# Routed experts of a decoder layer: weight pieces of 2048 columns, x turned after four contraction tiles, activations turned one block later

## The reference

```python
def expert_block(args):                      # xblk: up to 128 tokens of expert e
    xblk, e = args
    hid = jax.nn.silu(xblk @ w_gate[e]) * (xblk @ w_up[e])
    return hid @ w_down[e]
yb = lax.map(expert_block, (xb, block_e)).reshape(n_rows, d)
y = jax.ops.segment_sum(yb * row_w[:, None], row_tok, num_segments=t + 1)
```

## Time and profile before

| | |
|---|---|
| median of 3 runs | 2982.65 us (2980.33 to 2990.67) |
| the profiled execution, device time | 2996.13 us |
| its span in the trace | 2994.6 us |
| stretch with the experts' gate and up matmuls | 1879.7 to 2922.6 us |
| TensorE busy in the whole span | 84% |
| VectorE, ScalarE, GpSimd busy in the whole span | 61%, 42%, 28% |

### The profile page before, as it was taken

One profiled execution on the slowest core, in us unless ns is written; L12 is line 12 of the kernel. 1 busy time (PEld: TensorE's weight loads), 2 busy tenths in 40 slices (PEclk: granted clock), 3 DMA queues, 4 the chain that ended last, 5 costly groups with the idle time before them and its releaser, 6 DMA issues. The chain is left out here.

```text
span 2994.6 us, 38917 instructions
## 1 busy us (share of the span) xinstructions
PE 2519.6 (84%) x12384; PEld 2055.2 (69%) x12385; DVE 1819.8 (61%) x2399; ACT 1264.9 (42%) x1673; POOL 841.4 (28%) x895
## 2 busy tenths in 40 slices
PE   7989998998999899969978831799898988989891
PEld 6768777777877777847857721577777776777680
DVE  3346887787788655536546621666656667656744
ACT  3343453354345333334222100566656566555640
POOL 2012111221211111100002071444444444444442
PEclk8989999999999999989989875899999999999995
DMA  5423345442323353263543245778888889878954
GB/s 114 67 41 63 68 45 54 64 58 50 74 54 50 71 78 78 57 206 111 169 161 105 68 40 106 258 242 269 257 251 257 264 288 299 248 220 248 309 126 140
DMA packets 244044, 428.85 MB, mean 143 GB/s; under 512 B 26393, under 2 KB 150809, under 8 KB 243935
## 3 DMA queue, kind: packets, MB, share of 16 engines
q1 hardware_dynamic: 209566, 343.36, 42.6%
q0 software_dynamic: 34368, 84.02, 12.1%
HBM read 366.16 MB, written 93.58 MB: 154 GB/s over the span
## 5 line engine op out<-in xcount | busy, mean ns | idle before, releaser
L58 PE MATMUL dn_pj<-x_hi,dn_hi 128*128 128x512 f32 x1024 | 440.6, 430 | 4.1 <-PEq L83 2.2
L60 PE MATMUL dn_pj<-x_hi,dn_lo 128*128 128x512 f32 x1024 | 412.4, 403 | 0.0
L59 PE MATMUL dn_pj<-x_lo,dn_hi 128*128 128x512 f32 x1024 | 411.4, 402 | 0.0
L1007 DVE SCALAR_TENSOR_TENSOR uc_half<-u_in,par,uc_half 128x512 f32<-128x512 f32 x480 | 383.2, 798 | 13.1
L2247 DVE TENSOR_TENSOR e_lo<-e_raw,e_hi 128x1024 fp32r<-128x1024 f32 x256 | 337.1, 1374 | 73.0 <-ACT e_hi L2190 65.3
L58 PE MATMUL gu_ps<-e_hi,xg_hi 128*128 128x512 f32 x744 | 326.2, 438 | 56.2 <-DVE xg_lo L2252 33.7
L2190 ACT ACTIVATE e_hi<-e_raw 128x1024 fp32r<-128x1024 f32 x256 | 253.2, 1052 | 162.5 <-DMA e_raw<-in_w_gate_e_dram 130.3
L60 PE MATMUL gu_ps<-e_hi,xg_lo 128*128 128x512 f32 x744 | 307.3, 413 | 0.0
L59 PE MATMUL gu_ps<-e_lo,xg_hi 128*128 128x512 f32 x744 | 306.7, 412 | 0.0
L1146 POOL TENSOR_TENSOR a_lvl<-a_t,lvl_mask 128x512 f32<-128x512 f32 x112 | 167.7, 1514 | 353.1 <-PE dn_a L685 223.5
L60 PEld LDWEIGHTS dn_pj<-x_hi,dn_lo 128*128 128x128 f32 x1024 | 199.4, 195 | 46.4
(11 more groups left out here) (343 smaller groups left out, 5172.0 us busy)
## 6 DMA issues: line engine op xcount, KB each, us to landing
e_raw<-in_w_gate_e_dram SPq DMA_DIRECT2D x128, 512.0 KB
e_raw<-in_w_up_e_dram SPq DMA_DIRECT2D x128, 512.0 KB
e_raw<-in_w_down_e_dram SPq DMA_DIRECT2D x128, 512.0 KB
dn_raw<-in_w_in_dram SPq DMA_DIRECT2D x64, 512.0 KB
gate_rows<-qkv_next SPq DMA_DIRECT2D x16, 512.0 KB, 3.6
br_raw<-in_w_oa_dram SPq DMA_DIRECT2D x16, 512.0 KB
br_gate<-gate_rows SPq DMA_DIRECT2D x32, 256.0 KB, 4.2
br_raw<-in_w_ob_dram SPq DMA_DIRECT2D x16, 512.0 KB
```

What stands on the lines that cost most here:

```text
L58: nc.tensor.matmul(out, w_hi, x_hi, start=first, stop=False)
L59: nc.tensor.matmul(out, w_hi, x_lo, start=False, stop=False)
L60: return nc.tensor.matmul(out, w_lo, x_hi, start=False, stop=last)
L1007: ins = stt(out=uc[:], in0=u_in[:, t:t + HALF], scalar=w, in1=uc[:], op0=ALU.mult, op1=ALU.add)
```

## The change

It does five things in `experts`.

1. `raw` becomes three pieces of 2048 columns: gate and up of tiles 0 to 3, gate and up of tiles 4 to 7, and both halves of down. SP still issues six DMAs of 512 KB for an expert, two into each piece, and waits once for each piece. ScalarE and VectorE split a piece with one instruction.
2. Down weights are split one expert ahead instead of two, with semaphores of their own, and `down` waits for them. SP loads gate and up of expert e before down of e-1.
3. TensorE turns the next block's x after tiles 0 to 3. The activations are turned at the same place of the next block; the wait for `hid_s` stands in front of gate|up. Inside a group of three experts the two register loads of the next expert stand after the x transposes.
4. ScalarE's order in a block: piece 0, hi of the activations of the block before, first half of x, piece 1, silu, second half of x, piece 2, `y_move` of the block before.
5. VectorE's order: piece 0, lo of the activations, first half of x, `hidden`, second half of x, pieces 1 and 2.

At the start, only gate and up of experts 0 and 1 and down of expert 0 are split ahead of the loop. The rest of the program is as it was. GpSimd's program differs by the names of the register loads alone.

```diff
...
-            PIECES = 6
+            GU = 2
             BUFS = 3
-            SLOTS = 6
             LAG = 4
-            raw = [sb(ctx, f"e_raw{q}", [P, 4 * FF]) for q in range(SLOTS)]
+            raw = [sb(ctx, f"e_raw{i}", [P, 2, 4 * FF]) for i in range(GU + 1)]
...
-                if i < 4:
-                    ks, w = slice(4 * (i // 2), 4 * (i // 2) + 4), i % 2
-                    return raw[i][:].rearrange("p (k f) -> p k f", k=4), wh[j][:, ks, w, :], wl[j][:, ks, w, :]
-                return raw[i][:], dh[j][:, i - 4, :], dl[j][:, i - 4, :]
+                if i < GU:
+                    wkf = lambda w: w[j][:, 4 * i:4 * i + 4, :, :].rearrange("p k w f -> p w k f")
+                    return raw[i][:].rearrange("p w (k f) -> p w k f", k=4), wkf(wh), wkf(wl)
+                return raw[i][:], dh[j][:], dl[j][:]
...
-                def load(e, first):
-
-                    for i in range(PIECES):
+                def load_gate_up(e, first):
+
+                    for i in range(GU):
                         if not first:
-                            sp.wait_ge(lo_s, e * PIECES + (i + 1 - SLOTS))
-                        r = piece(0, i)[0]
-                        if i < 4:
-                            w = (a["w_gate_e"], a["w_up_e"])[i % 2]
-                            k0 = 4 * (i // 2)
-                            sp.dma_start(r, w[0, bass.ds(e, 1)].rearrange("o (p k) f -> p (o k) f", k=KT)
-                                         [:, k0:k0 + 4, :]).then_inc(w_in[i], 16)
-                        else:
-                            sp.dma_start(r, a["w_down_e"][0, bass.ds(e, 1)].rearrange("o (c p) n -> p (o c) n", p=P)
-                                         [:, i - 4, :]).then_inc(w_in[i], 16)
-
-                load(0, True)
-                with sp.Fori(1, E) as e:
-                    load(e, False)
+                            sp.wait_ge(lo_s, e * GU + (i + 1 - GU))
+                        for n, w in enumerate((a["w_gate_e"], a["w_up_e"])):
+                            src = w[0, bass.ds(e, 1)].rearrange("o (p k) f -> p (o k) f", k=KT)[:, 4 * i:4 * i + 4, :]
+                            sp.dma_start(raw[i][:, n, :].rearrange("p (k f) -> p k f", k=4), src).then_inc(w_in[i], 16)
+
+                def load_down(e, first):
+
+                    if not first:
+                        sp.wait_ge(dlo_s, e)
+                    for n in range(2):
+                        src = a["w_down_e"][0, bass.ds(e, 1)].rearrange("o (c p) n -> p (o c) n", p=P)[:, n, :]
+                        sp.dma_start(raw[GU][:, n, :], src).then_inc(w_in[GU], 16)
+
+                load_gate_up(0, True)
+                load_down(0, True)
+                load_gate_up(1, False)
+                with sp.Fori(2, E) as e:
+                    load_gate_up(e, False)
+                    load_down(e - 1, False)
+                load_down(E - 1, False)
...
-                def down(j, gb):
+                def down(e, j, gb):
+                    pe.wait_ge(dlo_s, e + 1)
                     pe.wait_ge(hl_s, gb + 1)
                     pe.wait_ge(y_ready, gb + LAG)
...
                 def hid_t(gb):
-                    pe.wait_ge(hid_s, gb + 1)
...
-                def blk(e, j, j_prev, gb, first):
-
-                    pe.wait_ge(xl_s, gb * 2 + 1)
-                    if first:
-                        pe.wait_ge(lo_s, e * PIECES + 2)
-                    gate_up(j, range(0, 4))
-                    pe.wait_ge(xl_s, gb * 2 + 2)
-                    if first:
-                        pe.wait_ge(lo_s, e * PIECES + 4)
-                    gate_up(j, range(4, 6))
-                    transposes(gb + 1)
-                    gate_up(j, range(6, 8)).then_inc(gu_done, 1)
-                    if j_prev is not None:
-                        down(j_prev, gb - 1)
-                    hid_t(gb)
-
-                def expert(e, j, nth, more):
-                    nb, base = plan(pe, e)
-                    blk(e, j, (j + BUFS - 1) % BUFS if not isinstance(e, int) or e > 0 else None, base, True)
-                    with pe.If(nb > 1):
-                        with pe.Fori(1, nb) as b:
-                            blk(e, j, j, base + b, False)
+                def run(experts):
+                    nb, base = blocks(pe, experts[0][0]), first_block(pe, experts[0][0])
+                    for i, (e, j, _) in enumerate(experts):
+                        following = experts[i + 1][0] if i + 1 < len(experts) else None
+                        loaded = []
+
+                        def blk(b, gb, first):
+                            prev = not first or not isinstance(e, int) or e > 0
+                            if prev:
+                                pe.wait_ge(hid_s, gb)
+                            pe.wait_ge(xl_s, gb * 2 + 1)
+                            if first:
+                                pe.wait_ge(lo_s, e * GU + 1)
+                            gate_up(j, range(0, 4))
+                            if prev:
+                                hid_t(gb - 1)
+                            pe.wait_ge(xl_s, gb * 2 + 2)
+                            transposes(gb + 1)
+                            if first:
+                                if following is not None:
+                                    loaded.extend((blocks(pe, following), first_block(pe, following)))
+                                pe.wait_ge(lo_s, e * GU + 2)
+                            gate_up(j, range(4, 8)).then_inc(gu_done, 1)
+                            if prev and first:
+                                down(e - 1, (j + BUFS - 1) % BUFS, gb - 1)
+                            elif prev:
+                                down(e, j, gb - 1)
+
+                        expert(pe, e, nb, base, blk)
+                        if following is not None:
+                            nb, base = loaded
...
-                    act.wait_ge(w_in[i], (nth * BUFS + j) * 16 + 16)
-                    A(h, r, ACT.Copy).then_inc(hi_s, 1)
+                    act.wait_ge(w_in[i], (nth * BUFS + j) * 32 + 32)
+                    A(h, r, ACT.Copy).then_inc(hi_s if i < GU else dhi_s, 1)
...
-                def blk(gb, prev, split):
-
-                    split(0, 1, 2, 3)
-                    act.wait_ge(gu_done, gb + 1)
-                    A(sg[:], gu[:, 0, :], ACT.Silu).then_inc(sg_s, 1)
-                    for b in range(2):
-                        act.wait_ge(t_done, gb * 2 + 5 + b)
-                        x_hi(b)
-                    if prev:
-                        y_move(gb - 1)
-                    act.wait_ge(ht_done, gb + 1)
-                    A(hh[:], ht[:], ACT.Copy).then_inc(hh_s, 1)
-                    split(4, 5)
...
+                def run(experts):
+                    for e, j, nth in experts:
+                        nb, base = blocks(act, e), first_block(act, e)
+
+                        def blk(b, gb, first):
+                            def split(i):
+                                ahead = 2 if i < GU else 1
+                                if first and (not isinstance(e, int) or e + ahead < E):
+                                    hi((j + ahead) % BUFS, nth + (j + ahead) // BUFS, i)
+
+                            prev = not first or not isinstance(e, int) or e > 0
+                            split(0)
+                            if prev:
+                                hid_hi(gb - 1)
+                            act.wait_ge(t_done, gb * 2 + 5)
+                            x_hi(0)
+                            split(1)
+                            act.wait_ge(gu_done, gb + 1)
+                            A(sg[:], gu[:, 0, :], ACT.Silu).then_inc(sg_s, 1)
+                            act.wait_ge(t_done, gb * 2 + 6)
+                            x_hi(1)
+                            split(2)
+                            if prev:
+                                y_move(gb - 1)
+
+                        expert(act, e, nb, base, blk)
...
-                def blk(e, b, gb, split):
-                    split(0, 1, 2, 3)
-                    dve.wait_ge(sg_s, gb + 1)
-                    v.scalar_tensor_tensor(out=hid[:], in0=sg[:], scalar=self.wt_tab[:, bass.ds(e * NT + b, 1)],
-                                           in1=gu[:, 1, :], op0=ALU.mult, op1=ALU.mult).then_inc(hid_s, 1)
-                    x_lo(gb + 1, 0)
-                    x_lo(gb + 1, 1)
+                def hid_lo(gb):
...
+                def run(experts):
+                    for e, j, _ in experts:
...
+                            split(0)
+                            if not first or not isinstance(e, int) or e > 0:
+                                hid_lo(gb - 1)
+                            x_lo(gb + 1, 0)
+                            dve.wait_ge(sg_s, gb + 1)
+                            v.scalar_tensor_tensor(out=hid[:], in0=sg[:], scalar=self.wt_tab[:, bass.ds(e * NT + b, 1)],
+                                                   in1=gu[:, 1, :], op0=ALU.mult, op1=ALU.mult).then_inc(hid_s, 1)
```

(57 more changed lines are left out.)

52 lines of the change are left out of this document (28 added, 24 removed).

## The result

The changed kernel takes **3071.3 us** (median of 4 runs, 3055.6 to 3074.9) against 2981.5 us for the kernel before in the same comparison: a ratio of **1.029, interval 1.025 to 1.032**. The forecast was 2957 us, range 2905 to 3000 us. It is wrong in sign and outside the range.

A forecast was written before the change was run, and what follows sets the result against it. TensorE set a floor of 858 us, with the splitting engines binding runs of one-block experts. Terms 23 - 30 - 9 - 7 - 3 = -26 us, from a median of 2982.65, gave 2957 us, range 2905 to 3000.

The forecast's parts named there:

- first to first: Silu-to-silu steps in runs of one-block experts: 35 steps, from 12.7 to 13.4 us each, +23 us.
- out of a run: Step from the last block of a one-block-expert run to a later block: 15 steps at 8.4 us, -30 us.
- later to first: Step from an expert's later block to the next expert's first block: 25 steps at 10.0 us, -9 us.
- lone first to later: Step from a first block outside such runs to a later block: 11 steps at 9.45 us, -7 us.
- Down starts about 1 us late, covered by the same loop: TensorE's down matmuls: `hid_lo` ready only after piece 0's remainder, about 1 us late, at no extra cost.
- The loop: Piece 1 freed, loaded, hi, silu, `hidden`, second x half, lo, freed: 13.4 us, with 7.5 from freed to full.
- well over 100: Sign of being right: ScalarE's wait for weights' DMA grows from 34 us to this, in front of the piece-1 copy.
- The slower rival: Piece 1's wait ahead of silu, its second half full only 8.8 us after freeing: 3002 us, chance 0.27.
- The start: Before the first silu: two pieces of 1024 fewer stand ahead, 2 to 4 us, taken as -3 us.
- the count of waits costs nothing: SP: same six DMAs but three waits instead of six, no cost; it already waits 434 us for VectorE.
- The third rival: TensorE's register loads left bare, 1.1 us in 17 or so first blocks, 19 us: 2976 us, chance 0.13.

The follow-up runs named there:

- a_1024: The changed kernel's order with six pieces of 1024 columns, each half with its own load, hi copy, subtraction and semaphore: ratio 1.013 to the kernel before.
- a_y_later: The changed kernel with `y_move` taken one block later on ScalarE, behind the activations' hi part and first half of x, ahead of piece 1 and silu: ratio 1.017.
- a_1024_y_pl: a_1024_y with GpSimd reading the next expert's registers behind the store of its first block, instead of ahead of the next gather: ratio 0.987, 2942.8 us.
- a_x6: The changed kernel with the x transposes back behind tile 5 and the register loads ahead of the wait for x: ratio 1.031.
- a_lo_halves: The changed kernel with VectorE's subtraction of each 2048-column piece made as two of 1024: ratio 1.025.
- a_p1: The changed kernel with ScalarE splitting piece 1 after silu and the second half of x: ratio 1.027.
- b_2048: The kernel before with three pieces of 2048 columns alone, in the old order, down still two experts ahead: ratio 1.014.
- b_2048_lo: b_2048 with each subtraction made as two of 1024 columns: ratio 1.001 to the kernel before.
- a_y_lo: The edits of a_lo_halves and a_y_later together on the changed kernel; loads, hi copies and semaphores still by 2048: ratio 1.009.
- a_pair: The changed kernel with hi copies and subtractions by halves of 1024 with own semaphore counts; SP still loads and frees by 2048: ratio 1.021.
- best_loads: a_1024_y_pl with TensorE's register loads of the following expert back in front of its first block, instead of behind the x transposes: ratio 0.986.
- b_pl: The kernel before with GpSimd's register loads placed behind the store: ratio 0.995.
- a_1024_y: The edits of a_1024 and a_y_later together on the changed kernel: ratio 0.994.

## Why the prediction was wrong

The steps between silus, sorted as in the prediction, from each profile's own starts:

| us | first to first (35) | out of a run (15) | later to first (25) | lone first to later (11) | all 92 |
|---|---|---|---|---|---|
| before | 446 | 156 | 259 | 111 | 1030 |
| forecast | 469 | 126 | 250 | 104 | 1007 |
| after | 470 | 163 | 290 | 121 | 1103 |
| a_1024 | 448 | 154 | 293 | 109 | 1064 |
| a_y_later | 448 | 180 | 271 | 116 | 1072 |
| a_1024_y_pl | 403 | 164 | 252 | 106 | 981 |

(The forecast's 1007 is 1030.5 with its four terms, 23 - 30 - 9 - 7.)

**Later to first: the step that failed.** I put "`y_move` is then at about +3.5 to +4", on the ground that GpSimd "was late, since its copy waits for the x transposes" and would start 1.4 us earlier. In the trace above it is at +7.7 (2090.12 against 2082.45), and on average over all 26 such steps (the table leaves one out) at +5.7, where the kernel before has +4.1. The rest of the reckoning held: 5.9 us of ScalarE's work and gaps stand between `y_move` and silu, and 5.7 + 5.9 is the 11.6 us that these steps take. So the term was 40 us too little for the 25 steps.

The store that `y_move` waits for is not issued 1.4 us earlier but 2.3 us later: 1.5 us ahead of silu on average, where the kernel before has 3.8 us (its 19 such steps with this wait). From the issue to `y_move` it takes no longer, 7.1 us against 8.4. GpSimd's loop has grown in two places. With the transposes no longer the last to come, its copy waited 185 us for the gather's landing (a_x6: moving them back changes nothing that can be measured). And I costed the 2048-column subtraction on VectorE alone, where on GpSimd it lengthened idx_gather from 298 to 715 ns, late_rows 423 to 641, idx_scatter 207 to 499 and x_gather 1289 to 1567, some 1.2 us for each block. The second is not what keeps these steps long, though: in a_lo_halves the copies are short and the store is issued at -3.7 us again, but then `y_move` follows 9.3 us after the issue, at +5.5, and the 26 steps sum to 298 us against 302. What does shorten them is to take either `y_move` one block later (a_y_later, 271 us in the table) or piece 1 behind silu (a_p1). Why the store takes longer when it is issued sooner stays open.

The Trainium skill, "SBUF — State Buffer" (Who interferes with whom), says that a VectorE instruction with two SBUF inputs contends with a GpSimd instruction that reads SBUF, because its second input comes through a read interface that the two share. The trace agrees: 2.32 us for one column beside the 2.28 us subtraction. I hadn't weighed it, and it spoke against this change; by the runs it is worth 1.3% in the old order (b_2048 to b_2048_lo), 0.8% with `y_move` moved (a_y_lo), and 0.4% or nothing in the changed order.

**"Down starts about 1 us late, covered by the same loop"** is the second. TensorE waited 157 us for hid_lo, with holes of 3 to 4 us. In steps from a first block to a later one, where silu mostly waits for TensorE, the hole is on its path: 2.2 us a step out of a run, 2.6 us in the lone ones. In the other steps silu waits for ScalarE, as shown above, and the hole counts only where it holds up `y_move`. After such a hole the down matmuls ran slower: 472, 450 and 449 ns on average against 390 ns in the kernel before, with a granted clock of 0.50, the lower level of 1.2 GHz, from 2111.8 to 2117.0 us, behind the hole of 3.93 us shown above. Most of this slow time only changed its place, since the gate|up matmuls became faster: their busy time fell from 940 to 891 us, that of the down matmuls rose from 435 to 510. I had moved the activations to the next block in the plan of TensorE and priced their 0.13 us; on ScalarE the same move put them behind `y_move` and piece 0, and closer to their use by half a gate|up. a_y_later takes `y_move` from ahead of them and wins 1.2%.

**Out of a run**, 37 us too low, is the same error: "down already ran while silu was late". It hadn't, since hid_lo was late as well. Lone first to later (17 us too low) is the same late chain.

**First to first** came out at 470 us for a forecast of 469, and that is luck. The place was right: in 28 of the 35 steps silu starts right behind ScalarE's own work, the copy of piece 1. The wait was not. The loop puts some 4.5 us a step in front of piece 1, for its load; there ScalarE waits 25 us in all 35 steps. It waits 105 us in front of `y_move` (70 for the store, 35 for the down matmuls), 16 for piece 0 and 25 for piece 2, 4.9 us a step in sum, and everything after is pushed on to silu. Its waits for weights in the whole stretch rose to 93 us (50.1 + 43.1), not "well over 100" in front of piece 1. A number that fits shows nothing of its cause. The slower rival, which had 0.27, ended on the right side for the same wrong reason.

**The start** was 5 us longer rather than 3 shorter: fewer bytes stand before silu, but ScalarE waited 7.3 us there for a piece of 2048.

**SP.** I had "the count of waits costs nothing", and freeing by 2048 columns was taken to lie in the loop. Loads and frees by halves win 0.8% (a_pair to a_1024), so the grain of SP's work has a price; which of the two carries it is not told apart.

**The third rival**, bare register loads, doesn't occur: in the profile after, TensorE's idle time after issue in front of gate|up matmuls is 2.6 us in 7 holes, 0.5 us at most, not 1.1 us each, and best_loads finds no change either. The durations held too: 1.91 us for a 2048-column hi copy, and 2.39 us on average for the subtraction, against 2.4.

What stays open: which of the kept parts (down one expert ahead, the order of x halves) gives the mended order its 0.8% over b_pl, and the intervals of a_lo_halves and a_pair overlap, so the first two of the three shares of the size are only roughly told apart. The sums of steps come from one profile for each kernel; that of the changed kernel lies 16 us under its median, so differences of a few us between rows say little.

## What to carry to other kernels

When an instruction is made longer, look at who shares a port with it before counting what is saved on its own engine: in the old order 2048-column subtractions saved 0.1 to 0.2 us each (2.29 us against twice 1.22) and cost 1.3% (b_2048 against b_2048_lo), as GpSimd's copies grew longer, and halves gave it back. When an operation is moved, follow it in every engine's order, not only in that of the engine which waits: what it now stands behind sets its time. Here a late store held `y_move`, and with it all that stood behind it on ScalarE up to silu. In a loop of several engines a wait that is removed is replaced by the next (here hid_lo, then x_gather), so two mends can be worth more together (3.5%) than apart (1.6 and 1.2%).

## What the runs showed of the hardware

- A GpSimd copy of one uint32 column took 2.32 us while VectorE subtracted 2048 columns from two SBUF tiles (2.28 us), and 0.18 us a moment later.
- The pair of register reads on GpSimd costs 2.08 us ahead of its next copy in the trace; placed behind a DMA issue, where the engine waits anyway, it is mostly hidden: that idle time falls from 135.2 to 42.4 us (a_1024_y to a_1024_y_pl).
- An accumulating indirect store issued at 2094.27 us, with a gather and weight loads under way, held up `y_move` until 2105.57 us, 11.3 us; the one issued at 2082.95 us did so for 7.2 us.
